# A 31-tap convolution on TensorE: from two token phases to four, in an eight-core encoder block

## The chip, the cores and the metric

The kernel runs as one program on all 8 cores of one Trainium2 chip, each core on its own sequences and with no exchange between cores. The time is the device time of the slowest core, in microseconds (us); lower is better.

## What is computed

A pre-normalised mixer layer, applied to 8 long sequences (8192 tokens) and 32 short ones (2048 tokens) of width 1024. One input projection of 3584 columns feeds two groups of 512 channels; their outputs are joined, projected back, gated and added to the residual, and a last RMSNorm follows.

```python
h = rmsnorm(x, norm_g) * (1.0 + scale[:, None, :]) + shift[:, None, :]
p = h @ w_in                                              # (B, L, 3584)
a_in, a_b, a_c, a_z, b_v, b_g, b_z = jnp.split(p, SPLITS, axis=-1)
y_a = a_b * dwconv(a_c * a_in, conv_a_w) * jax.nn.silu(a_z)          # 3 taps
u = b_v * jax.nn.sigmoid(b_g)
u = dwconv(u, conv_b_w) + conv_b_b                                   # 31 taps, each channel by itself
y_b = jax.nn.silu(head_layernorm(u, ln_g, ln_b)) * jax.nn.silu(b_z)  # norm over groups of 64 channels
y = jnp.concatenate([y_a, y_b], axis=-1) @ w_out                     # (B, L, 1024)
out = rmsnorm(x + gate[:, None, :] * y, final_g)
```

## The kernel before

**Windows and periods.** A core has 16 windows of 1024 tokens: eight of its long sequence, then two for each of four short ones. A window's tokens are split by parity into q = 0 and q = 1, 512 each. Period w of the loop does the input projection of window w, and beside it the long convolution, the norm and the output projection of window p = w - 1. Period 0 and `period_last` (w = 15, which also finishes its own window) have code of their own.

**Slots.** The order of work on every engine is written out by hand. A period has 28 slots; each slot is two `mm1` calls (L521), and each of these is 8 matmuls of 128 x 128 weights and 512 columns (L525). Slots 0 to 7 give the gated product u, 8 to 15 the input of the short convolution, 16 to 19 and 24 to 27 its gates, 20 to 23 the gate of group B (`zb`). After slot 21 comes `stage_d(p, 0)`, after slot 27 `stage_d(p, 1)`: the output projection (L757), 64 matmuls each. Two dictionaries hang further work on the slots: `mid` runs between the two `mm1` of a slot, `post` behind the slot. Each engine works its queue in order.

**The long convolution.** u is written to DRAM (`u_scratch`, L554), with 8 edge columns to the neighbouring windows (the halo; for a window with two neighbours one DMA, L561, otherwise L565). `vread(p, j)` reads it back as V, so that a row of V holds one channel at one shift: 16 channels x 8 shifts make the 128 rows; two DMAs of 64 rows each (L638). There are two V buffers; `vread` of j = 0 and 1 is issued after slots 4 and 5, of j = 2 and 3 after the first burst of convolution matmuls. `conv_b` (L642) does one of eight units u: 4 steps x 4 column positions, each 32 columns of weights (16 channels x 2 phases) against 512 tokens (L648). Four units (`conv4`) follow on each other as one burst of 64 matmuls, after slot 9 and after slot 15. Unit u needs V(u // 2).

**The norm.** ACT copies a unit's result with its bias to `sq` (L656), DVE adds four units (`add4`, L663), one matmul with Bn gives the mean (L671), DVE centres (L680), ACT squares, DVE adds, one matmul with Bm gives the variance (L689). ACT takes Ln and Exp (L698, L699), DVE multiplies (L709), ACT does silu (L712), POOL multiplies by the gate in YP (L714). `norm_hooks` (L831) sets the slots.

**Moves.** `g_move` (L583) brings the gate from `gst` to YP in the row order of the convolution, `y_move` (L726) the product from YP to yB in the order of the output projection. Both issue on SP, as do the loads of x (L308, L736), the transposes of the scaled rows to hT (L345), the stores of y (L813) and, in the periods 2 to 9, the preparation of gated output weights. `conv_a` (L594) is the short convolution: four operations of 512 columns on DVE. The squares of the last norm are ACT's (L786), and DVE's L795 and POOL's L797 wait for them.

## Time and profile before

| | us |
|---|---|
| median of 3 runs | 2233.69 (2232.13 to 2260.23) |
| the profiled execution | 2235.12 |
| its slowest core, from first to last instruction | 2233.5 (cores: 2220.0 to 2233.5) |
| PE busy | 2165.8 |
| DVE busy | 1326.2 |
| ACT busy | 980.0 |
| POOL busy | 628.2 |

The profile is that of core 3. PE (TensorE) is the busiest engine by far; a matmul's own duration (380 ns for 512 columns) includes its run through the array, and a stream of them steps faster than that. So the time of a stream is read from the starts of its first matmul and of the next line's first. "SPq" and "ACTq" rows are DMA issues on these engines' queues; their landing times stand in the answers on a line. A wait is put down to what ended last by the profile.

### The profile page before, as it was taken

The page shows a single profiled execution, that of the slowest core. Times are in us where ns is not written, and L with a number is a line of the kernel's source. Part 1 is how long each engine was busy: PE and PEld are TensorE (multiplying, and loading weights), DVE is VectorE, ACT ScalarE, POOL GpSimd, SP SyncE. Part 2 cuts the span into 40 slices and gives each one's busy share as a digit, 9 for nine tenths or more (in the row PEclk, how much of TensorE's full clock was granted, in tenths as well). Part 3 has the DMA queues.
Part 4 walks back from the last instruction along what each step waited for, and adds up shares of the span by engine and source line. Part 5 has one row for each costly group of instructions (what it writes and reads, how often), then busy time and mean ns, then how long its engine had stood idle before and what let it go on. Part 6 is the DMA issues. An engine that isn't in the chain of part 4 may idle for free.

```text
span 2233.5 us, 38878 instructions; the slowest of 8 cores (2220.0 to 2233.5 us)
## 1 busy us (share of the span) xinstructions
PE 2165.8 (97%) x11524; PEld 963.5 (43%) x11524; DVE 1326.2 (59%) x2251; ACT 980.0 (44%) x1644; POOL 628.2 (28%) x564
## 2 busy tenths in 40 slices
PE   4998999999999999999999999999999999999997
PEld 1443444444444444444444444444444444444443
DVE  1245574656657556476655747566575665647578
ACT  2232626345263443535435263443626445263464
POOL 3223324223242331423313242131311312122123
PEclk9999999999999999999999999999999999999999
DMA  9977477786766878668676777567565766656666
GB/s 259 155 212 192 131 186 197 201 199 183 190 188 197 212 183 175 174 191 236 180 202 175 195 229 209 153 185 171 168 187 154 195 196 155 187 128 204 159 180 223
DMA packets 300314, 418.49 MB, mean 187 GB/s; under 512 B 168616, under 2 KB 225104, under 8 KB 291920
## 3 DMA queue, kind: packets, MB, share of 16 engines
q1 hardware_dynamic: 291712, 408.50, 68.0%
q0 software_dynamic: 7392, 7.34, 2.6%
q8 instruction: 101, 1.65, 0.3%
q14 instruction: 101, 0.83, 0.1%
q10 hardware_dynamic: 1008, 0.17, 0.0%
HBM read 265.43 MB, written 92.82 MB: 160 GB/s over the span
## 4 chain that ended last, share of the span: by engine, by line
PE 88%; DMA 6%; DVE 2%; issue 1%; SPq 1%; ACT 1%; POOL 0%; DVEq 0%; POOLq 0%; ACTq 0%
PE pb L525 64%; PE pb L757 19%; PE pb L648 4%; DMA xb<-w_out 3%; DMA u_scratch<-u 1%; DMA V<-w_ada 1%; DMA w_in_sb<-w_in 1%; DVE sq L663 1%; SPq L393 0%; ACT sq L656 0%; PE pb L671 0%; PE pb L689 0%; DVE hT L386 0%; SPq L345 0%; DVE xb L810 0%
## 5 line engine op out<-in xcount | busy, mean ns | idle before, releaser
L525 PE MATMUL pb<-hT,w_in_sb 128*128 128x512 bf16 x7168 | 1578.5, 380 | 16.6 <-DMA w_in_sb<-w_in 9.7
L525 PEld LDWEIGHTS pb<-hT,w_in_sb 128*128 128x128 bf16 x7168 | 699.3, 98 | 875.9 <-issue 46.6
L531 ACT ACTIVATE tp<-pb 128x512 f32<-128x512 f32 x384 | 227.0, 595 | 618.3 <-PE pb L525 566.8
L768 DVE TENSOR_TENSOR xb<-pb,xb 128x512 f32<-128x512 f32 x252 | 171.4, 689 | 197.2 <-PE pb L757 185.3
L786 ACT ACTIVATE tp<-xb 128x1024 bf16<-128x1024 f32 x126 | 133.4, 1059 | 314.0 <-DVE xb L768 218.6
L757 PE MATMUL pb<-w_out_sb,yB 128*128 128x512 bf16 x960 | 251.2, 379 | 4.5
L757 PE MATMUL pb<-w_out_sb,yA 128*128 128x512 bf16 x960 | 246.3, 379 | 3.0 <-DVE xb L768 1.9
L797 POOL TENSOR_TENSOR rsE<-msE,mhalf 128x1 f32<-128x1 f32 x128 | 139.5, 1090 | 385.8 <-DVE msE L795 368.4
L324 POOL TENSOR_TENSOR rsA<-msA,mhalf 128x2 f32<-128x2 f32 x64 | 46.2, 722 | 649.9 <-DVE msA L322 649.9
L605 DVE SCALAR_TENSOR_TENSOR tp<-t,caT_sb,tp 128x512 f32<-128x512 bf16 x256 | 195.3, 763 | 28.4 <-DVE tp L602 1.4
L534 DVE TENSOR_TENSOR t<-pb,tp 128x512 bf16<-128x512 f32 x128 | 88.3, 690 | 160.7 <-PE pb L525 116.2
L714 POOL TENSOR_TENSOR YP<-tp,YP 128x512 bf16<-128x512 f32 x128 | 149.2, 1198 | 120.6 <-ACT tp L712 120.6
L316 ACT ACTIVATE tp<-xb 128x1024 bf16<-128x1024 f32 x128 | 134.9, 1055 | 95.9 <-DMA xb<-x 76.2
L551 DVE SCALAR_TENSOR_TENSOR u<-tp,pb 128x512 bf16<-128x512 f32 x128 | 87.7, 685 | 142.2 <-PE pb L525 141.8
L810 DVE SCALAR_TENSOR_TENSOR xb<-xb,rsE,fg_bc 128x1024 f32<-128x1024 f32 x125 | 162.7, 1303 | 6.2 <-POOL rsE L797 4.2
L329 POOL TENSOR_SCALAR xs<-xb,rsA 128x1024 bf16<-128x1024 f32 x128 | 144.6, 1141 | 14.7 <-POOL rsA L324 14.7
L663 DVE TENSOR_TENSOR sq<-sq 128x512 bf16<-128x512 bf16 x192 | 98.7, 527 | 82.5 <-ACT sq L656 75.6
L757 PEld LDWEIGHTS pb<-w_out_sb,yB 128*128 128x128 bf16 x960 | 91.8, 98 | 124.7 <-issue 18.4
L757 PEld LDWEIGHTS pb<-w_out_sb,yA 128*128 128x128 bf16 x960 | 93.7, 98 | 116.8 <-issue 4.2
L534 DVE TENSOR_TENSOR ga<-pb,tp 128x512 bf16<-128x512 f32 x128 | 87.6, 685 | 70.4 <-PE pb L525 64.5
L680 DVE SCALAR_TENSOR_TENSOR pb<-pb,cbb_sb,tp 128x512 f32<-128x512 f32 x128 | 87.5, 752 | 63.6 <-ACT tp L673 63.6
L503 POOL TENSOR_TENSOR xb<-xb 128x1024 bf16<-128x1024 f32 x32 | 76.9, 2408 | 147.9 <-DMA xb<-w_out 147.9
(102 smaller groups left out, 1308.2 us busy)
## 6 DMA issues: line engine op xcount, KB each, us to landing
xb<-x SPq DMA_DIRECT2D x254, 512.0 KB, 7.9
V<-u_scratch SPq DMA_DIRECT2D x128, 527.5 KB, 9.0
y<-xb SPq DMA_DIRECT2D x126, 512.0 KB, 3.9
xb<-w_out SPq DMA_DIRECT2D x40, 512.0 KB, 12.8
YP<-gst SPq DMA_DIRECT2D x64, 256.0 KB, 5.0
yB<-YP SPq DMA_DIRECT2D x120, 128.0 KB, 3.0
u_scratch<-u SPq DMA_DIRECT2D x80, 130.0 KB, 3.6
wg_scratch<-xb SPq DMA_DIRECT2D x32, 256.0 KB, 9.5
```

Source lines behind the costliest of these rows:

```text
L316: T.op("scalar", lambda e: e.activation(out=jb[:].bitcast(BF16), in_=xbuf[:], func=AF.Square, accum_out=ssA[:, c:c + 1]), reads=[xkey], wr ...
L329: T.op("gpsimd", lambda e, xbuf=xbuf, sub=sub, r=r: e.tensor_scalar(out=xs[:, sub, :], in0=xbuf[:], scalar1=rsA[:, r:r + 1], scalar2=1.0, ...
L525: T.op("tensor", lambda e, bank=bank, kc=kc: e.matmul(bank[:], lhsT=w_in_sb[:, kc, col0:col0 + 128], rhs=hT2[q][:, kc, :], start=(kc == 0) ...
L531: T.op("scalar", lambda e: e.activation(out=t[:], in_=bank[:], func=func, scale=scale), reads=[bkey], writes=[tkey])
L534: T.op("vector", lambda e: e.tensor_tensor(out=dst, in0=bank[:], in1=t[:], op=ALU.mult), reads=[tkey, bkey], writes=[dkey])
L605: T.op("vector", lambda e, k=k: e.scalar_tensor_tensor(out=acc[:], in0=terms[k], scalar=caT[:, j * KA + k:j * KA + k + 1], in1=acc[:], op0 ...
L714: T.op("gpsimd", lambda e, t=t, u=u: e.tensor_tensor(out=YP[:, u, :], in0=t[:], in1=YP[:, u, :], op=ALU.mult), reads=[tkey, ("yp", u, 0), ...
L757: T.op("tensor", lambda e, kc=kc, src=src: e.matmul(bank[:], lhsT=src, rhs=w_out_sb[:, kc, h * NT:(h + 1) * NT], start=(kc == 0), stop=(kc ...
L768: T.op("vector", lambda e, bank=bank, xbuf=xbuf, h=h: e.tensor_tensor(out=xbuf[:, h * NT:(h + 1) * NT], in0=bank[:], in1=xbuf[:, h * NT:(h ...
L786: T.op("scalar", lambda e: e.activation(out=jb[:].bitcast(BF16), in_=xbuf[:], func=AF.Square, accum_out=ssE[:, c:c + 1]), reads=[xkey], wr ...
L797: T.op("gpsimd", lambda e: e.tensor_tensor(out=rsE[:, c:c + 1], in0=msE[:, c:c + 1], in1=mhalf[:, 0:1], op=ALU.pow), reads=[("msE", c), "m ...
L810: T.op("vector", lambda e: e.scalar_tensor_tensor(out=xbuf[:], in0=xbuf[:], scalar=rsE[:, c:c + 1], in1=fg_bc[:], op0=ALU.mult, op1=ALU.mult),
```

## The change

**Four phases.** Tokens are split by their remainder mod 4. V holds 8 channels x 16 shifts in its rows, a matmul's 32 weight columns are 8 channels x 4 phases, and it covers 256 tokens. A unit is now 2 halves x 3 steps x 4 column positions, 24 matmuls of 256 columns; a burst (`conv_quad`) is 96. All four banks of a burst are taken first, and the four copies by ACT stand behind all matmuls; the bias is no longer added there but, centred beforehand, in `ln_center` (`center_bias` in period 0).

**Places.** The bursts stand after slots 8 and 14. The mean of the first stays two slots behind its burst and that of the second goes half a slot further behind; the second `add4` and all that follows come one slot later against the burst, so that they end at slots 15 and 21 as before.

**DMAs.** A V load is four pieces of 32 rows instead of two of 64. u goes out as two pieces per row, the halo is 4 columns for each of them, and a window with two neighbours has two halo DMAs. `y_move` is 16 DMAs of 64 KB a window instead of 8 of 128 KB, half of a quad's in `mid`, half in `post`. `g_move` is 16 DMAs of 64 KB on ACT's queue instead of 4 of 256 KB on SP's.

**Smaller operands.** Mean, variance, Ln, Exp and their copies have 256 columns. `add4` has one more addition of 256 columns; centring and silu are done in halves; `conv_a` has five operations (two of 512 columns, two of 256, one of 512). The ring TP has 4 buffers instead of 6, beside a new ring MR of two half-size ones; the ring of u has 3 instead of 4. Some constants of the start share memory with yA, and the table of taps loaded at the start is 384 KB instead of 128 KB.

The core of the diff (the host's reordering of channels, the constants and `period_last` are left out; of the two bursts that `period_last` has for its own window the second goes half a slot earlier, and the norm of both goes up to one output step later):

```diff
 def second_of(kind, w, q, j):
-                sides = ([] if wfirst[w] else [(w - 1, PAD + NT, PAD)]) + ([] if wlast[w] else [(w + 1, 0, NT)])
-                if len(sides) == 2:
...
+                sides = ([] if wfirst[w] else [(w - 1, PAD + NB, PAD)]) + ([] if wlast[w] else [(w + 1, 0, NB)])
+                for k, (ww, c, m) in enumerate(sides):
+                    T.dma("sync", lambda e, ww=ww, c=c, m=m: e.dma_start(out=u_rows(ww, q, j, c, PAD), in_=ub[:, :, m:m + PAD]),
+                          reads=[ukey], writes=[("Uh", q, j, w, ww)], semkey=("uh", ww > w) + ukey)
 def g_move(q):
-            for h in range(2):
-                T.dma("sync", lambda e, h=h: e.dma_start(out=YP[q::2, h::2, :], in_=gst[64 * h:64 * h + 64, :, :]),
+            for u in range(8):
+                T.dma("scalar", lambda e, u=u: e.dma_start(out=YP[q::2, u, :], in_=gst[32 * (u % 4):32 * (u % 4) + 32, 2 * (u // 4):2 * (u // 4) + 2, :]),
 def vread(p, j):
+            for b in range(4):
+                k = b
+                src = U_d[p, j]
+                src = bass.AP(src.tensor, src.offset + k, [[VN, 32], [1, VN - k]])
+                T.dma("sync", lambda e, b=b, k=k, src=src: e.dma_start(
+                    out=buf[32 * b:32 * b + 32, :, :].rearrange("p g t -> p (g t)")[:, 0:VN - k], in_=src),
+                    reads=deps, writes=[(key, b)], semkey=("vl", key, b))
+        def conv_quad(p, hh):
+            us = quad(hh)
...
+                cst[u] = list(PB.next(pin=True))
+            for u, h, a, g in itertools.product(us, range(2), range(3), range(4)):
+                vb, vkeys = V[u]
+                bank, bkey = cst[u]
+                j, G = u // 2, 8 * (u % 2) + 4 * h + g
+                T.op("tensor", lambda e, vb=vb, bank=bank, g=g, h=h, a=a, j=j, G=G: e.matmul(
+                    bank[32 * g:32 * g + 32, NB * h:NB * h + NB], lhsT=WC[:, 64 * a + 16 * j + G, :], rhs=vb[:, G * VW + 4 * a:G * VW + 4 * a + NB],
+                    start=(a == 0), stop=(a == 2), tile_position=(0, 32 * g)),
+                    reads=[("WC", 2 * a + j // 2)] + vkeys, writes=[bkey], signal=(a == 2 and h == 1 and g == 3))
...
+                T.op("scalar", lambda e, bank=bank, vv=vv: e.activation(out=vv[:], in_=bank[:], func=AF.Copy), reads=[bkey], writes=[vvkey])
 def norm_hooks(hh, h, mid, post):
             add(mid, h + 1, lambda: add4(quad(hh)))
-            add(mid, h + 2, lambda: conv_mean(hh))
-            add(mid, h + 2, lambda: ln_center(hh))
-            add(mid, h + 3, lambda: add4(quad(hh)))
-            add(mid, h + 4, lambda: ln_var(hh), lambda: ln_act(hh))
-            add(mid, h + 5, lambda: fin2(hh, 0))
-            add(post, h + 5, lambda: fin2(hh, 1))
+            add(post if hh else mid, h + 2, lambda: conv_mean(hh), lambda: ln_center(hh))
+            add(mid, h + 4, lambda: add4(quad(hh)))
+            add(post, h + 5, lambda: ln_var(hh), lambda: ln_act(hh))
+            add(mid, h + 6, lambda: fin2(hh, 0))
+            add(post, h + 6, lambda: fin2(hh, 1))
 def conv_hooks(p, mid, post):
             add(post, 4, lambda: vread(p, 0))
             add(post, 5, lambda: vread(p, 1))
-            for hh, h in enumerate((9, 15)):
-                add(post, h, lambda hh=hh: conv4(p, hh))
+            for hh, h in enumerate((8, 14)):
+                add(post, h, lambda hh=hh: conv_quad(p, hh))
                 if hh == 0:
                     add(post, h, lambda: vread(p, 2), lambda: vread(p, 3))
                 norm_hooks(hh, h, mid, post)
-                add(post, h + 6, lambda hh=hh: y_move(hh, yb))
+                add(mid, h + 7, lambda hh=hh: y_move(quad(hh)[:2], yb))
+                add(post, h + 7, lambda hh=hh: y_move(quad(hh)[2:], yb))
```

On PE, one period from its first slot on, before (L525 are the projection's matmuls, 8 for half a slot; L648 the convolution; L671 and L689 mean and variance):

```order
L525 MATMUL pb<-hT,w_in_sb 128x512 x224
L648 MATMUL pb<-V,WC 32x512 x64
L525 MATMUL pb<-hT,w_in_sb 128x512 x24
L671 MATMUL pb<-sq,Bn 128x512
L525 MATMUL pb<-hT,w_in_sb 128x512 x32
L689 MATMUL pb<-sq,Bm 128x512
L525 MATMUL pb<-hT,w_in_sb 128x512 x40
L648 MATMUL pb<-V,WC 32x512 x64
L525 MATMUL pb<-hT,w_in_sb 128x512 x24
L671 MATMUL pb<-sq,Bn 128x512
L525 MATMUL pb<-hT,w_in_sb 128x512 x32
L689 MATMUL pb<-sq,Bm 128x512
```

and after, where the same lines are L545, L677, L703 and L723:

```order
L545 MATMUL pb<-hT,w_in_sb 128x512 x208
L677 MATMUL pb<-V,WC 32x256 x96
L545 MATMUL pb<-hT,w_in_sb 128x512 x24
L703 MATMUL pb<-sq,Bn 128x256
L545 MATMUL pb<-hT,w_in_sb 128x512 x56
L723 MATMUL pb<-sq,Bm 128x256
L545 MATMUL pb<-hT,w_in_sb 128x512 x16
L677 MATMUL pb<-V,WC 32x256 x96
L545 MATMUL pb<-hT,w_in_sb 128x512 x32
L703 MATMUL pb<-sq,Bn 128x256
L545 MATMUL pb<-hT,w_in_sb 128x512 x48
L723 MATMUL pb<-sq,Bm 128x256
```

Each burst stands 16 matmuls of 512 columns earlier and has 96 entries. Counted from the burst's end, the first mean stays 24 behind, the second goes from 24 to 32, and both variances stand farther behind their means.

On SP, in a period whose window has two neighbours, around the loads for the first burst, before (L554 writes u, L561 the halo to both sides, L638 loads V, L308 loads x; L491 and L497 prepare output weights):

```order
L554 DMA u_scratch<-u 128x512
L561 DMA u_scratch<-u 128x2x8
L638 DMA V<-u_scratch 64x1x4220 x2
L554 DMA u_scratch<-u 128x512
L561 DMA u_scratch<-u 128x2x8
L638 DMA V<-u_scratch 64x1x4220 x2
L308 DMA xb<-x 128x1024
L554 DMA u_scratch<-u 128x512
L561 DMA u_scratch<-u 128x2x8
L491 DMA xb<-gate_scratch 128x1024
L497 DMA xb<-w_out 128x1024
L554 DMA u_scratch<-u 128x512
```

and after (L579, L583, L663, in the same order of names):

```order
L579 DMA u_scratch<-u 128x2x256
L583 DMA u_scratch<-u 128x2x4 x2
L663 DMA V<-u_scratch 32x4224
L663 DMA V<-u_scratch 32x4223
L663 DMA V<-u_scratch 32x4222
L663 DMA V<-u_scratch 32x4221
L579 DMA u_scratch<-u 128x2x256
L583 DMA u_scratch<-u 128x2x4 x2
L663 DMA V<-u_scratch 32x4224
L663 DMA V<-u_scratch 32x4223
L663 DMA V<-u_scratch 32x4222
L663 DMA V<-u_scratch 32x4221
```

V(0) and V(1) keep their places among the writes of u, as four issues each.

On ACT, after slot 21 and through the first output projection, after the change (L597 is the gate of group B, L602 `g_move`, L821 the squares of the last norm):

```order
L597 ACTIVATE gst<-pb 128x2x256 x2
L602 DMA YP<-gst 64x1x512 x8
L821 ACTIVATE tp,ssE<-xb 128x1024 x4
L597 ACTIVATE gst<-pb 128x2x256 x4
L602 DMA YP<-gst 64x1x512 x8
L551 ACTIVATE tp<-pb 128x512
```

The eight issues of `g_move` stand ahead of the four squares, where before ACT had none: there SP issued `g_move` as two DMAs behind the transposes.

## Rows read from the trace of the kernel before

**Rows 1.** The page: busy time by engine; the chain that ended last, by engine

```profile
PE 2165.8 (97%) x11524; PEld 963.5 (43%) x11524; DVE 1326.2 (59%) x2251; ACT 980.0 (44%) x1644; POOL 628.2 (28%) x564
PE 88%; DMA 6%; DVE 2%; issue 1%; SPq 1%; ACT 1%; POOL 0%; DVEq 0%; POOLq 0%; ACTq 0%
```

**Rows 2.** Waits of PE: line waited for, us in total, times, longest

```profile
PE pb L671 <- DVE sq L663: 8.4, 4, 2.6
PE pb L525 <- DVE hT L386: 5.9, 3, 2.6
```

**Rows 3.** Timeline of PE, period 7: start, us, line, operands, count

```profile
1034.64 8.80 PE L525 MATMUL pb<-hT,w_in_sb 128*128 128x512 bf16 x40
1043.37 3.64 PE L648 MATMUL pb<-V,WC 128*32 128x512 bf16 x64
1046.94 3.41 PE L525 MATMUL pb<-hT,w_in_sb 128*128 128x512 bf16 x15
```

**Rows 4.** Matmul groups by form: count, busy us, mean ns, idle before, releasers

```profile
L671 PE MATMUL pb<-sq,Bn 128*128 128x512 bf16 x32 | 12.1, 379 | 8.5 <-DVE sq L663 8.4 <-PE pb L525 0.2
...
L359 PE MATMUL pb<-yA,xs 128*128 128x128 bf16 x64 | 4.9, 219 | 0.3
```

**Rows 5.** Weight loads by form, same columns

```profile
L648 PEld LDWEIGHTS pb<-V,WC 128*32 128x32 bf16 x2048 | 51.8, 97 | 62.3 <-issue 13.6
...
L359 PEld LDWEIGHTS pb<-yA,xs 128*128 128x128 bf16 x64 | 3.8, 97 | 4.4 <-issue 3.9
```

**Rows 6.** Timeline of PE at the start, transposes

```profile
66.46 0.61 PE L359 MATMUL pb<-yA,xs 128*128 128x128 bf16 x8
```

**Rows 7.** Timeline of SP's DMA issues, period 10

```profile
1398.72 0.42 SPq L565 DMA_DIRECT2D u_scratch<-u  x1
...
1402.83 1.26 SPq L638 DMA_DIRECT2D V<-u_scratch  x2
...
1406.23 1.29 SPq L638 DMA_DIRECT2D V<-u_scratch  x2
```

**Rows 8.** V loads: first bursts of periods 1 and 15, second of period 6

```profile
L638 SPq DMA_DIRECT2D V<-u_scratch x4: 523/574/1007, 190.7 to 195.1; - x4
...
DMA to landing us min/median/max: 5.0/7.8/8.5
...
L638 SPq DMA_DIRECT2D V<-u_scratch x4: 520/529/567, 2068.6 to 2072.7; - x4
...
DMA to landing us min/median/max: 5.1/6.7/8.5
...
L638 SPq DMA_DIRECT2D V<-u_scratch x4: 515/518/851, 885.5 to 892.2; - x4
...
DMA to landing us min/median/max: 11.6/13.2/14.2
```

**Rows 9.** Timeline of PE, the bursts that needed these loads

```profile
205.69 3.64 PE L648 MATMUL pb<-V,WC 128*32 128x512 bf16 x64
...
2083.73 3.64 PE L648 MATMUL pb<-V,WC 128*32 128x512 bf16 x64
...
905.80 3.64 PE L648 MATMUL pb<-V,WC 128*32 128x512 bf16 x64
```

**Rows 10.** Timeline of SP's DMA issues, end of period 0

```profile
163.22 1.25 SPq L583 DMA_DIRECT2D YP<-gst  x2
164.66 6.78 SPq L345 DMA_TRANSPOSE hT<-xs  x4
```

**Rows 11.** Timeline of ACT: a DMA issue at the start; first square of period 9

```profile
17.08 0.59 ACTq L246 DMA_DIRECT2D lnb_sb<-lnbT  x1
...
1343.22 1.06 ACT L786 ACTIVATE tp<-xb 128x1024 bf16<-128x1024 f32 x1 [7.79 <-DVE xb L768]
```

**Rows 12.** Timelines of SP and of PE at the end

```profile
2200.64 3.00 SPq L726 DMA_DIRECT2D hT<-YP  x4
...
2205.76 3.18 PE L757 MATMUL pb<-w_out_sb,hT 128*128 128x512 bf16 x14
```

**Rows 13.** DVE groups by form, the long operation of the short convolution

```profile
L605 DVE SCALAR_TENSOR_TENSOR tp<-t,caT_sb,tp 128x512 f32<-128x512 bf16 x256 | 195.3, 763 | 28.4 <-DVE tp L602 1.4
```

More of the change, by code:

```diff
@@ L1 @@
 import contextlib
+import itertools
 import numpy as np
@@ L255, in build_nc @@
         T.op("gpsimd", lambda e: e.memset(ones1[:], 1.0), writes=["ones1"])
[L256 to L260 removed]
+        T.op("vector", lambda e: e.memset(scT, 0.0), writes=["scT"])
+        for i in range(3):
             T.op("gpsimd", lambda e, i=i: e.memset(UR.bufs[i][:], 0.0), writes=[("u", i)])
@@ L434, in gate_piece @@
                 gate_st["bank"] = PB.next(pin=True)
-                gate_st["bias"] = TP.next(pin=True)
+                gate_st["bias"] = (early[:, 256:512], "gbias")
                 bb, bk = gate_st["bias"]
@@ L632, in vread @@
             T._need("sync", T._deps("sync", [], VK["V%d" % key[1]]))
-            for par in range(2):
-                q = 1 - par
-                deps = [("U", q, j, p)] + ([] if wfirst[p] else [("Uh", q, j, p - 1)]) + ([] if wlast[p] else [("Uh", q, j, p + 1)])
-                src = U_d[p, par, j]
-                src = bass.AP(src.tensor, src.offset + par, [[VN, 16], [1, 4], [1, VN - 4]])
-                T.dma("sync", lambda e, par=par, src=src: e.dma_start(
-                    out=buf[64 * par:64 * par + 64, :, :].rearrange("p g t -> p (g t)")[:, 0:VN - 4], in_=src),
-                    reads=deps, writes=[(key, par)], semkey=("vl", key, par))
@@ L642, in conv_b @@
-        def conv_b(p, u):
-            j, hl = u // 2, u % 2
-            vb, vkey = vst[(p, j)]
-            bank, bkey = PB.next(pin=True)
-            for s in range(4):
-                for g in range(4):
-                    T.op("tensor", lambda e, s=s, g=g: e.matmul(
-                        bank[32 * g:32 * g + 32, :], lhsT=WC[:, (4 * u + g) * 4 + s, :], rhs=vb[:, 4 * hl + g, 4 * s:4 * s + NT],
-                        start=(s == 0), stop=(s == 3), tile_position=(0, 32 * g)),
-                        reads=[("WC", u // 2)] + [(vkey, k) for k in range(2)], writes=[bkey], signal=(s == 3 and g == 3))
-            if hl == 1:
-                VR.unpin(vkey)
-                vst.pop((p, j))
-            vv, vvkey = sqr.next(pin=True)
-            T.op("scalar", lambda e: e.activation(out=vv[:], in_=bank[:], func=AF.Identity, bias=cbb[:, u:u + 1], scale=1.0),
-                 reads=[bkey, "cbb"], writes=[vvkey])
-            cst[u] = [bank, bkey, vv, vvkey]
+            deps = []
@@ new lines, in vread @@
+            for q in range(2):
+                deps += [("U", q, j, p)] + ([] if wfirst[p] else [("Uh", q, j, p - 1, p)]) + ([] if wlast[p] else [("Uh", q, j, p + 1, p)])
+            for b in range(4):
[5 more added lines that the diff above has]
+                    reads=deps, writes=[(key, b)], semkey=("vl", key, b))
@@ L663, in add4 @@
                 T.op("vector", lambda e, x=x, y=y: e.tensor_tensor(out=x[:], in0=x[:], in1=y[:], op=ALU.add), reads=[xk, yk], writes=[xk])
+            x, xk = a
+            for n in (NB,):
+                T.op("vector", lambda e, n=n: e.tensor_tensor(out=x[:, 0:n], in0=x[:, 0:n], in1=x[:, n:2 * n], op=ALU.add), reads=[xk], writes=[xk])
         def quad(hh):
@@ L670, in conv_mean @@
             mb, mbk = PB.next()
-            T.op("tensor", lambda e: e.matmul(mb[:], lhsT=Bn[:], rhs=vv[:], start=True, stop=True), reads=["Bn", vvkey], writes=[mbk])
-            m, mkey = TP.next(pin=True)
-            T.op("scalar", lambda e: e.activation(out=m[:], in_=mb[:], func=AF.Copy), reads=[mbk], writes=[mkey])
+            T.op("tensor", lambda e: e.matmul(mb[:, 0:NB], lhsT=Bn[:], rhs=vv[:, 0:NB], start=True, stop=True), reads=["Bn", vvkey], writes=[mbk])
+            m, mkey = MR.next(pin=True)
+            T.op("scalar", lambda e: e.activation(out=m[:], in_=mb[:, 0:NB], func=AF.Copy), reads=[mbk], writes=[mkey])
             cst[("m", hh)] = (m, mkey)
@@ L688, in ln_var @@
             vb, vbkey = PB.next(pin=True)
-            T.op("tensor", lambda e: e.matmul(vb[:], lhsT=Bm[:], rhs=vv[:], start=True, stop=True), reads=["Bm", vvkey], writes=[vbkey])
+            T.op("tensor", lambda e: e.matmul(vb[:, 0:NB], lhsT=Bm[:], rhs=vv[:, 0:NB], start=True, stop=True), reads=["Bm", vvkey], writes=[vbkey])
             for u in quad(hh):
```

326 lines of the change are left out of this document (178 added, 148 removed).

## The prediction

> **What bounds the kernel now.** I read the page first: PE is busy 97% of the span and the chain that ended last is 88% PE [rows 1], so time is gained only by shortening PE's stream or by taking away what it waits for. The list of PE's waits comes next: outside the start, PE waits for the sums ahead of the mean matmul and for the modulated rows hT [rows 2]. The timeline of a steady period then shows PE running without a gap: 40 matmuls of 512 columns from 1034.64 to 1043.37 us, 0.218 us each, then the 64 convolution matmuls, 3.57 us from the first to the next line's first [rows 3]. So a term counts fully if it lies in PE's stream, and anything else only once PE has to wait for it.
>
> **The convolution, 64 x 512 columns to 96 x 256.** Four matmuls with different column positions run together: 64 matmuls in 3.57 us are 16 groups of four at about 0.216 us, and 3.57 - 16 x 0.216 = 0.12 us around the burst. So four tiles together cost what one 512-column matmul costs. For 256 columns there is no row in bf16. The nearest is the transposes of 128 columns: eight in 0.61 us, of which the last alone has 219 ns [rows 4, 6], so (0.61 - 0.219) / 7 = 56 ns each. Halfway between 56 (128 columns) and 216 (512) by column count, 56 + (216 - 56) / 3 = 109, say 110 ns. The new burst has 24 groups: 24 x 0.110 + 0.12 = 2.76 us, 0.81 less; 32 bursts give **-25.9 us**. The bound on the other side is a group that takes its weight load in full: the loads of this line take 97 ns each [rows 5], 97 + 110 = 207 ns a group, 24 x 0.207 + 0.12 = 5.09 us, +1.52 x 32 = +48.6. The saving is zero at 16 x 0.216 / 24 = 144 ns a group. I take 110, because the transposes, each with a weight load of 97 ns of its own, step at 56 ns [rows 5, 6]: loads overlap there even where they are longer than the matmul.
>
> The page of the Trainium skill "TensorE: Matmul & The Clock Gate", Part 3, "The mechanism", speaks against the change: a weight load overlaps running matmuls only where the row group differs, and here every load uses all 128 rows. By that rule the burst would be the 5.09 us of the upper bound. The present trace does not follow it: transposes on all 128 rows step faster than one load lasts.
>
> **Mean and variance.** The 32 mean matmuls [rows 4] and as many variance matmuls go from 512 to 256 columns: 64 x (0.216 - 0.110) = **-6.8 us**. Their operands are one addition longer on DVE.
>
> **Waits for the sums.** The 8.4 us in four waits [rows 2] average 2.1. They stand at the second burst of periods with w_out preparation, where the mean now comes half a slot (8 matmuls of 0.216, 1.73 us) later against its burst; one more half-size addition eats some 0.3. Left are about 4 x 0.7: **-5** (0 to -8.4).
>
> **Start of period 1.** On SP the transposes (164.66 us) stood behind g_move (163.22, two issues of 0.6) [rows 10], and PE waits 5.9 us for their rows [rows 2]. g_move is now on the ACT queue, and the transposes no longer stand behind its wait: **-4** (0 to -8).
>
> **V loads, the new exposure.** Bursts move up one slot (16 x 0.216 = 3.45 us); V(0) and V(1) are still issued after slots 4 and 5, in the middle of the u writes [rows 7], and the data is as late as before. V(1) is needed by the third of four units. Before, that was 1.73 us behind the burst's start; now it is 3.45 earlier plus two units of 6 groups, 12 x 0.110 = 1.31: 2.14 us *before* the old start. Last landings against the old start: in period 1 195.1 + 8.5 = 203.6 against 205.69, -2.1; in period 15 2072.7 + 8.5 = 2081.2 against 2083.73, -2.5 [rows 8, 9]; all fifteen, read the same way: -2.1, -0.4, -0.9, -1.1, -1.3, +0.9, -1.8, -2.5, -1.7, -1.9, -1.4, -1.9, -2.2, -1.4, -2.5. On top come 0.47 us for the second halo DMA ahead of it on SP (0.42 each plus the step) [rows 7] in periods 1 to 6, and an estimated 0.3 because the last of four issues of some 0.55 replaces the last of two, in a queue that is backed up 8 us anyway. Wait = landing + delay + 2.14, where positive: 12.7 us in periods 1 to 6, 4.9 after: **+17.6**. Bounds: 9 if the delays are nil and the four pieces land sooner; 35 if every early period is like the sixth (6 x 3.8) and the others lose 1.3 each. PE's stream is in order, so nothing else fills these waits.
>
> The second burst moves as well. Its loads follow the first burst's release of V and usually land some 8 us ahead, but in period 6 the last lands at 892.2 + 14.2 = 906.4 at most (905.6 by its own issue) against 905.80 [rows 8, 9]. Four such periods (2, 3, 5, 6) could lose up to 2.9 each, 9.6 together; most of it is the same backlog that the first burst's wait already gave time to drain: **+3.5**.
>
> **Moved DMA issues.** g_move on ACT is 16 issues a window of 0.4 to 0.6 us [rows 11]. The first eight are queued behind slot 21's activations and ahead of four squares; ACT idled 7.79 us before the first of these (1343.22) [rows 11]. Four units can go at once, 2.4 us; the other four wait for y_move's landing, some 3 us after its last issue, and end near 1343.4: covered, barely. The second eight stand ahead of slot 24's copies, 4.8 us in which PE fills three of eight banks. Behind the first stand the squares, DVE's scale of them waits for these, and PE would wait for banks only after that. Taken as **0** (0 to +15, one us a period). y_move has 16 issues instead of 8; its first half goes out half a slot earlier, and the transposes behind it have all of slots 22 to 27 as cover: 0. conv_a gains one half-size operation on DVE, about 0.4 us of L605's 763 ns [rows 13] against a slot of 3.45; DVE is 59% busy, so it delays the last u by up to 1 us, which is inside the V range. The split of silu and of the centring adds instructions on ACT (44%) and DVE, with no PE wait near it.
>
> **Tail.** The last window's y_move issues 3.00 us for four and PE continues at 2205.76 [rows 12]; eight issues are twice that, partly under 40 matmuls: **+3** (0 to 5).
>
> **Sum** against the profiled execution (2235.1 us, its slowest span 2233.5): -25.9 - 6.8 - 5 - 4 + 17.6 + 3.5 + 0 + 3 = -17.6, so 2217.5. The median of the runs is 1.4 below the profiled execution: **2216**.
>
> **Rivals.** *A, the V loads are covered after all*: 32-partition pieces land sooner, or a wait in one period lets the queue catch up for all later ones. For it: late periods have only 0 to 1 us to find. Against it: the loads are bound by the queue, and that moves the same bytes. Without the two V terms: 2216 - 21.1 = 2195. *B, the V loads take everything*: both bursts wait at their upper bounds (35 + 9.6), 2195 + 44.6 = 2240. For it: periods 2 to 6, where landings already come within a microsecond of the old start. Against it: from period 7 on PE has no other wait and the queue drains. *C, slower: the four-tile group does not get below 207 ns*, because weight loads or the issue of instructions set its pace. It decides at 144 ns. For it: a group is eight instructions, at 216 ns 27 ns each, and no row has a sustained pace above that; 110 ns needs 14. Against it: transposes step at the column count. 2216 + 25.9 + 48.6 = 2290; mean and variance stand alone among 512-column matmuls and keep their gain.
>
> **How the numbers follow.** Forecast (2203 to 2230) 0.66; A (2186 to 2203) 0.15; B (2230 to 2252) 0.13; C (2265 to 2300) 0.06. A change of 2%, about what a measurement of this kernel can tell from none, is 45 us: below 2189 or above 2278. Only the lower end of A is below, 0.05; C, for nearly all its width, is above, 0.06; the rest, 0.89, is in between. The range leaves out C, the lower end of A and the upper end of B: 2191 to 2243.
>
> **What would show it.** In the profile after: a burst of 96 with 2.76 us to the next line's first matmul (C: over 5); mean and variance steps of 0.11; a new line in PE's waits, convolution <- DMA V, of 15 to 20 us on the slowest core, mostly periods 1 to 6 (A: under 3; B: over 35, and on both bursts); the waits for sq and hT at half or less; late periods shorter by two bursts and four norm matmuls, 2 x 0.81 + 4 x 0.106 = 2.0 us, less the V wait. I am wrong if the squares on ACT start late by microseconds and PE then waits on banks, or if u itself comes late from DVE so that the V issues, not the landings, slip.

## The result and the profile after

The changed kernel takes 2365.72 us (median of 3 runs, 2364.77 to 2670.41) against 2233.69: **132 us slower**. The ratio is 1.055 with an interval of 1.0373 to 1.0726. The interval is wide because one of the three runs was disturbed and is left out. The forecast was 2216 (2191 to 2243), with 0.06 for slower.

The page after, busy time by engine and the chain that ended last, to be read against [rows 1]:

```profile
PE 2180.0 (92%) x12550; PEld 1005.6 (43%) x12550; DVE 1391.8 (59%) x2568; ACT 976.1 (41%) x1772; POOL 627.4 (27%) x564
PE 70%; DMA 15%; DVE 4%; SPq 4%; issue 3%; ACT 2%; POOL 0%; DVEq 0%; ACTq 0%; POOLq 0%
PE pb L545 49%; PE pb L792 18%; DMA V<-u_scratch 6%; DMA u_scratch<-u 5%; PE pb L677 3%; DMA xb<-x 2%; SPq L663 2%; DMA V<-w_ada 1%; DVE tp L628 1%; DVE sq L692 1%; DMA w_in_sb<-w_in 1%; DVE u L575 1%; SPq L579 1%; ACT sq L686 1%; SPq L583 1%
```

PE is no longer the whole chain: 15% of it is DMA, and the two transfers in it are u into DRAM and V out of it. The waits of PE (line waited for, us in total, times, longest), to be read against [rows 2], name the same pair:

```profile
PE pb L677 <- DMA V<-u_scratch: 87.3, 23, 8.5
PE pb L703 <- DVE sq L695: 13.6, 8, 4.2
PE pb L545 <- ACT tp L551: 12.2, 5, 4.2
PE pb L545 <- DVE hT L394: 7.5, 1, 7.5
PE pb L677 <- ACT tp L551: 3.8, 5, 1.0
```

The wait for V was forecast as 15 to 20 us; it is 87 on the slowest core (58 to 87 over the eight). The compute steps came out as worked out. This is PE's timeline (start, us, line, operands, count) of a second burst without stalls, where [rows 3, 9] show the old one:

```profile
1543.64 0.27 PE L723 MATMUL pb<-sq,Bm 128*128 128x256 bf16 x1
1543.75 3.62 PE L545 MATMUL pb<-hT,w_in_sb 128*128 128x512 bf16 x16
1547.30 2.81 PE L677 MATMUL pb<-V,WC 128*32 128x256 bf16 x96
1550.04 2.33 PE L545 MATMUL pb<-hT,w_in_sb 128*128 128x512 bf16 x10
```

The burst lasts 1550.04 - 1547.30 = 2.74 us (forecast 2.76), so a group of four tiles steps at about 110 ns; the variance matmul steps at 1543.75 - 1543.64 = 0.11 us.

**Where the time went**, slowest core against slowest core (2364.0 - 2233.5 = 130.5 us). PE's waits for V: +87.3. Waits for banks that ACT had not freed (L551, both lines): +16.0. Waits for sq: 13.6 - 8.4 = +5.2. Waits for hT rows: about +3. PE's own busy time: 2180.0 - 2165.8 = +14.2, although the burst and the norm became shorter. That is 126 of 130.5. The last term is the clock. In this table of PE's stretches on core 3 (stretch, length, busy, matmuls; granted clock, DMA share, GB/s), the stretch from 499.2 begins inside a stall of 7.20 us that lasts until 503.7:

```profile
490.00:499.00 9.00, 6.05 (x70) 1.00 1.06 152
499.20:509.30 10.10, 5.59 (x55) 0.50 0.99 205
509.40:515.00 5.60, 5.60 (x28) 1.00 0.95 173
```

PE's timeline of the same stretch (idle before and its releaser in brackets):

```profile
495.01 1.49 PE L677 MATMUL pb<-V,WC 128*32 128x256 bf16 x48 [0.45 <-DMA V<-u_scratch]
503.71 2.75 PE L677 MATMUL pb<-V,WC 128*32 128x256 bf16 x48 [7.20 <-DMA V<-u_scratch]
506.39 6.80 PE L545 MATMUL pb<-hT,w_in_sb 128*128 128x512 bf16 x24
```

PE first stood, then got 0.50 of full speed (1.2 of 2.4 GHz): its second half burst took 2.75 us for 48 matmuls where the first took 1.49. From 85 us on, stretches at 0.50 sum to 72 to 126 us a core after, and 12 to 23 before. The transfers around the stall keep the 16 engines busy throughout (shares of 1.06 and 0.99).

**Why V is late.** The rows of DMA issues give landing times (the last column, median us from issue to landing). Before:

```profile
u_scratch<-u SPq DMA_DIRECT2D x80, 130.0 KB, 3.6
u_scratch<-u SPq DMA_DIRECT2D x48, 128.0 KB, 4.8
u_scratch<-u SPq DMA_DIRECT2D x80, 2.0 KB, 3.3
u_scratch<-u SPq DMA_DIRECT2D x48, 4.0 KB, 4.6
```

After:

```profile
DMA packets 347188, 419.12 MB, mean 177 GB/s; under 512 B 199080, under 2 KB 271824, under 8 KB 338768
u_scratch<-u SPq DMA_DIRECT2D x80, 130.0 KB, 5.9
u_scratch<-u SPq DMA_DIRECT2D x48, 128.0 KB, 9.8
u_scratch<-u SPq DMA_DIRECT2D x176, 2.0 KB, 8.6
```

u holds two blocks of 256 columns a row now, so its pieces are 512 bytes instead of 1024 and those of the halo 8 instead of 16: the trace counts 22,528 packets of 16 bytes before and 45,056 of 8 bytes after. Bytes are the same, but u and its halo land in 6 to 10 us instead of 3 to 5. V itself lands no later after its issue (9.0 us before, 6.5 to 9.2 for its four pieces after); late against the burst, which itself comes a slot sooner, is its issue. SP waits for the halo before it may issue V, as it did before: its waits for u and halo sum to 90.5 us on core 3 before and 112.3 on core 5 after. Its timeline on core 5, to be read against [rows 7]:

```profile
495.93 0.88 SPq L583 DMA_DIRECT2D u_scratch<-u  x2
502.17 1.72 SPq L663 DMA_DIRECT2D V<-u_scratch  x4
503.99 0.38 SPq L579 DMA_DIRECT2D u_scratch<-u  x1
504.42 0.99 SPq L583 DMA_DIRECT2D u_scratch<-u  x2
505.68 1.72 SPq L663 DMA_DIRECT2D V<-u_scratch  x4
```

and PE's:

```profile
494.78 12.68 PE L545 MATMUL pb<-hT,w_in_sb 128*128 128x512 bf16 x58
512.13 2.75 PE L677 MATMUL pb<-V,WC 128*32 128x256 bf16 x48 [4.67 <-DMA V<-u_scratch]
```

After its halo issues SP stands from 496.81 to 502.17, then V(0), the next u and V(1) leave late, and PE waits 4.67 us for V(0) and 4.78 for V(1). Each piece of V now reads rows of both parities and so waits for the halo of both. That by itself moves nothing: before, the half of V that SP issues first waited for the odd parity, which is written last. The ring of u adds to it: in all, DVE waits 32.6 us for u buffers whose transfers haven't landed, where the row of before has no such wait.

### The profile page after: what moved, and what is told of

It is laid out like the page before. It is cut to its first block, busy times and chain, and to the rows that moved or that the text cites. A ratio compares the mean times of both kernels' runs of the same rounds, so it can differ in the third digit from the quotient of the medians.

```text
span 2364.0 us, 43369 instructions; the slowest of 8 cores (2334.0 to 2364.0 us)
## 1 busy us (share of the span) xinstructions
PE 2180.0 (92%) x12550; PEld 1005.6 (43%) x12550; DVE 1391.8 (59%) x2568; ACT 976.1 (41%) x1772; POOL 627.4 (27%) x564
## 2 busy tenths in 40 slices
DMA packets 347188, 419.12 MB, mean 177 GB/s; under 512 B 199080, under 2 KB 271824, under 8 KB 338768
## 4 chain that ended last, share of the span: by engine, by line
PE 70%; DMA 15%; DVE 4%; SPq 4%; issue 3%; ACT 2%; POOL 0%; DVEq 0%; ACTq 0%; POOLq 0%
PE pb L545 49%; PE pb L792 18%; DMA V<-u_scratch 6%; DMA u_scratch<-u 5%; PE pb L677 3%; DMA xb<-x 2%; SPq L663 2%; DMA V<-w_ada 1%; DVE tp L628 1%; DVE sq L692 1%; DMA w_in_sb<-w_in 1%; DVE u L575 1%; SPq L579 1%; ACT sq L686 1%; SPq L583 1%
## 5 line engine op out<-in xcount | busy, mean ns | idle before, releaser
L545 PE MATMUL pb<-hT,w_in_sb 128*128 128x512 bf16 x7168 | 1590.8, 383 | 32.8 <-ACT tp L551 12.2
L545 PEld LDWEIGHTS pb<-hT,w_in_sb 128*128 128x128 bf16 x7168 | 701.5, 98 | 894.2 <-issue 80.8
L551 ACT ACTIVATE tp<-pb 128x512 f32<-128x512 f32 x384 | 226.4, 594 | 636.4 <-PE pb L545 504.1
L821 ACT ACTIVATE tp<-xb 128x1024 bf16<-128x1024 f32 x126 | 133.2, 1057 | 298.3 <-DVE xb L803 210.0
L628 DVE SCALAR_TENSOR_TENSOR tp<-t,caT_sb,tp 128x256 f32<-128x256 bf16 (+2 forms) x384 | 228.2, 594 | 41.8 <-DVE tp L625 1.4
L677 PE MATMUL pb<-V,WC 128*32 128x256 bf16 x3072 | 114.0, 310 | 91.4 <-DMA V<-u_scratch 87.3
L337 ACT ACTIVATE tp<-xb 128x1024 bf16<-128x1024 f32 x120 | 126.4, 1054 | 84.2 <-DMA xb<-x 65.4
L677 PEld LDWEIGHTS pb<-V,WC 128*32 128x32 bf16 x3072 | 90.5, 108 | 118.0 <-issue 112.1
```

The costliest lines, as they stand in the source:

```text
L545: T.op("tensor", lambda e, bank=bank, kc=kc: e.matmul(bank[:], lhsT=w_in_sb[:, kc, col0:col0 + 128], rhs=hT2[q][:, kc, :], start=(kc == 0) ...
L551: T.op("scalar", lambda e: e.activation(out=t[:], in_=bank[:], func=func, scale=scale), reads=[bkey], writes=[tkey])
L628: T.op("vector", lambda e, k=k, dst=dst, src=src: e.scalar_tensor_tensor(out=dst, in0=src, scalar=caT[:, j * KA + k:j * KA + k + 1], in1=d ...
L677: T.op("tensor", lambda e, vb=vb, bank=bank, g=g, h=h, a=a, j=j, G=G: e.matmul(bank[32 * g:32 * g + 32, NB * h:NB * h + NB], lhsT=WC[:, 64 ...
L821: T.op("scalar", lambda e: e.activation(out=jb[:].bitcast(BF16), in_=xbuf[:], func=AF.Square, accum_out=ssE[:, c:c + 1]), reads=[xkey], wr ...
```

## Experiments

All ratios are to the kernel before, from runs on the same chip. Theories at the start: the earlier slots alone (the forecast's own term, larger than estimated); the u path, by SP's queue, by the V pieces, by the wait for both parities' transfers, or by the traffic of the small pieces; and the smaller rings (tp 6 to 4 with 2 small ones, u 4 to 3).

**Slots.** The change with its bursts back at 9 and 15, and the kernel before with its bursts at 8 and 14 (the hooks of the norm go with the slots):

```
-            for hh, h in enumerate((8, 14)):      # after_s915; norm_hooks as before
+            for hh, h in enumerate((9, 15)):
-            for hh, h in enumerate((9, 15)):      # before_s814; norm_hooks as in the change
+            for hh, h in enumerate((8, 14)):
```

> The change with its bursts back at slots 9 and 15 and the norm hooks of before (mean two slots, variance four slots behind the burst, y_move six); layout, pieces, queues and rings stay. Theory 1, the moved slot: every wait of the convolution for V shrinks by up to the slot, 3.45 us; the 60 to 90 us of these waits fall to 5 to 25 (periods 1 to 6 only), the low-clock stretches behind them go too, and the time falls to 2215 to 2270. Theory 2, the new data path (u, halo and V arrive microseconds later than the old ones, whatever the slot): waits of 3 to 4 us stay in most periods, 40 us or more in all, and the time stays over 2290. Theory 3, the smaller rings: waits for ACT's copies stay at 10 to 27 us, and the time stays over 2300.

> The kernel before with one thing changed: its bursts at slots 8 and 14 and the norm hooks of the change behind them (y_move still after slots 15 and 21). Theory 1, the moved slot alone costs what was seen: 60 us or more of waits for V, time over 2300. Theory 2, it is the new data path: by the landings of before, 15 to 25 us of waits for V, time 2245 to 2265. If V is hidden in the old layout: within 5 us of 2234.

Measured 1.0353 (1.0319 to 1.0387) and 1.012 (1.008 to 1.0161). In the kernel before, the earlier slot makes waits for V of 12.2 us on the slowest core, below the 21.1 of the forecast; in the change, most of the loss stays at the old slots. First the row of before_s814, then that of after_s915:

```profile
PE pb L648 <- DMA V<-u_scratch: 12.2, 6, 4.0
```

```profile
PE pb L677 <- DMA V<-u_scratch: 33.1, 10, 5.2
PE pb L703 <- DVE sq L695: 23.6, 9, 4.9
```

**Rings of the change in the kernel before** (tp 4 with two buffers for mean and rstd, u 3):

> The kernel before with the rings of the change: four buffers of tp and two of full size for mean and reciprocal instead of six for both, three buffers of u instead of four (gate bias and the squares of period 0 in yA1's memory, as in the change). Theory 3, the rings: a new line of PE waits for ACT's copies into tp, 10 us or more, time 2250 to 2270. Theories 1 and 2: within 8 us of 2234.

Measured 1.0041 (1.0004 to 1.0077). By themselves the rings cost the old kernel about 9 us (1 to 17).

**The pieces of V.** after_v128 loads V(j) by one DMA of 128 rows (and a tail), after_v64 by two of 64 rows:

```
+ full = bass.AP(src.tensor, src.offset, [[1, 4], [VN, 32], [1, VN - 3]])            # after_v128
+ half = bass.AP(src.tensor, src.offset + 2 * b, [[VN, 32], [1, 2], [1, n]])         # after_v64
```

> The change with V read by one DMA of 128 rows (4221 of 4224 columns) and a small one for the last three columns of the first 32 rows, instead of four DMAs of 32 rows; the bytes stay. Theory 4, pieces of 32 rows are slow: the second V lands 2 us sooner after its issue, waits for V fall by 20 to 35 us and the time to 2300 to 2330. Otherwise, if the pieces don't matter: within 10 us of 2366; one DMA that has to land whole may be later by up to 1 us a load, 2375.

> The change with V read by two DMAs of 64 rows, 32 runs outermost and two shifts inside, plus a small one for the last two columns, instead of four DMAs of 32 rows; the rows' order in V and in the table of weights follows. Theory 4, pieces of 32 rows are slow: the second V lands 1 to 2 us sooner, time 2325 to 2350. If pieces don't matter: within 10 us of 2366. Against the one DMA of 128 rows, whose outermost level has four steps (2869): if it was the number of outermost steps that spreads a load over the engines, this one with 32 steps must be back at 2380 or less.

Measured 1.2846 (1.2807 to 1.2885), 2864 us, with this row, and 1.0566 (1.049 to 1.0643), 2356 us:

```profile
PE pb L678 <- DMA V<-u_scratch: 330.4, 32, 16.5
```

The same bytes in one DMA with an outermost level of four steps wait 330 us; in two with 32 steps they cost what the change costs, within an interval of 34 us. So the size of V's pieces is not the cause.

**SP's queue.** s915_uact issues u and halo on ACT's queue instead of SP's, with the bursts at 9 and 15:

```
-  T.dma("sync", ...)     # u rows and halo
+  T.dma("scalar", ...)
```

> The change at slots 9 and 15 (after_s915) with the writes of u and of the halo issued on ACT's queue instead of SP's. Theory 2, these small writes are late because they stand in SP's ring behind stores of 512 KB and loads of V: on a ring of their own they land in 3 to 4 us, SP never stands in front of a V load, waits for V and for the sums fall under 15 us, time 2210 to 2245. Rival: ACT stands in its queue until DVE has written u, its copies come late, and PE waits for them; time 2290 or more. If the ring doesn't matter: within 10 us of after_s915 (2300).

Measured 1.0417 (1.0396 to 1.0438) against 1.0353 on SP. u and halo land about as late from another queue, so it is not SP's ring that makes them late. The run doesn't clear SP's issuing of all blame: on the slowest cores PE's wait for V falls from 33.1 to 20.2 us, while its waits for hT go from 9.0 to 26.0 and those for ACT's copies from 1.8 to 6.4, as the rival had it. Landings:

```profile
u_scratch<-u ACTq DMA_DIRECT2D x80, 130.0 KB, 6.0
u_scratch<-u ACTq DMA_DIRECT2D x48, 128.0 KB, 6.7
u_scratch<-u ACTq DMA_DIRECT2D x176, 2.0 KB, 6.8
```

**The u path alone.** before_upath gives the kernel before, in windows with two neighbours, u in two pieces of 512 bytes a row and two halo DMAs:

> The kernel before, slots and rings as they were, with u written in the pieces of the change in the six windows with two neighbours: two pieces of 512 bytes a row (the buffer has a gap between them) and two halo DMAs instead of one (16-byte pieces). Theory 2a, small pieces make u and halo late: their landing goes from 4 to 5 us in periods 2 to 6 to 8 to 10, SP stands in front of the V loads until they land, 20 to 40 us of new waits for V and for the sums, time 2255 to 2275. If pieces and number of DMAs don't matter: within 8 us of 2234.

Measured 1.0109 (1.0087 to 1.013): 24 us, by the same sign (u lands later, V is waited for). The halo has its 22,528 pieces of 16 bytes here as before; only u's pieces and the DMAs of the halo double in these windows. So u can land late without more or smaller pieces of the halo:

```profile
PE pb L655 <- DMA V<-u_scratch: 14.7, 5, 3.9
u_scratch<-u SPq DMA_DIRECT2D x48, 128.0 KB, 8.6
u_scratch<-u SPq DMA_DIRECT2D x176, 2.0 KB, 6.3
```

**The halo.** after_nohalo writes whole u rows with empty edges and no halo DMA, so the convolution lacks the neighbouring windows' columns. after_dummyhalo is the same with all halo DMAs issued into a scratch array that nobody reads:

```
-  sides = ...                                             # after_nohalo
-  for k, (ww, c, m) in enumerate(sides): T.dma("sync", ... out=u_rows(ww, q, j, c, PAD) ...)
+  lo, hi = 0, VW
-  ... out=u_rows(ww, q, j, c, PAD), in_=ub[:, :, m:m + PAD]      # after_dummyhalo, from after_nohalo
+  ... out=uh_rows(ww, q, j, c, PAD), in_=ub[:, :, m:m + PAD]
```

> The change without the halo: every window is padded with zeros as if it stood alone, no halo DMA is issued and V waits for none (the edges between windows are left out of the computation). Theory 2b, SP waits in front of the V loads until this period's halo has landed: periods 1 to 6 fall from 143 to 150 us to 134 to 138, time 2290 to 2320. Theory 1 alone (the loads themselves are too late for slot 8): V loads are issued where they were in the late periods and each period keeps 3 to 5 us of waits, 2320 to 2350. If the halo doesn't matter: over 2350.

> after_nohalo with the halo's DMAs issued again as in the change, same number, sizes and places on SP, but into a scratch tensor that nobody reads, so that no V load waits for them (the edges between windows are left out of the computation). Theory 2b, it is the wait of SP for this period's halo in front of the V loads: time as after_nohalo, 2260 to 2285. Theory 2c, it is the traffic of the small pieces itself: u's landing goes back from 4 to 6 to 10 us, periods 1 to 6 take over 142 us, time 2330 or more.

Measured 1.0177 (1.0149 to 1.0205), below both ranges expected, and 1.0475 (1.0453 to 1.0498). Without the halo, PE's wait for V on the slowest core is near the forecast (23.0 us, and 1.2 to 23.0 over the cores); the transfers alone, which nothing waits for but the u buffers, bring most of the time back. First after_nohalo, then after_dummyhalo:

```profile
PE pb L673 <- DMA V<-u_scratch: 23.0, 12, 3.6
u_scratch<-u SPq DMA_DIRECT2D x128, 132.0 KB, 3.9
```

```profile
PE pb L681 <- DMA V<-u_scratch: 49.2, 15, 5.7
u_scratch<-u SPq DMA_DIRECT2D x128, 132.0 KB, 5.9
```

So of 1.055, 0.037 (83 us) hang on the halo: 0.030 (66 us) on its traffic, and 0.0075 (17 us) on waiting for it. The interval of 1.055 is wide: the 83 us are good to about 40, and the 17 are not settled. With four u buffers (below), where the intervals are narrow, the halo costs 1.0448 - 1.014 = 0.031, 69 us.

**What in the traffic.** Three variants of after_dummyhalo: pieces of 64 bytes in the same number, one halo DMA instead of two in windows with two neighbours, and the same pieces into SBUF:

```
-  out=uh_rows(ww, q, j, c, PAD), in_=ub[:, :, m:m + PAD]
+  out=uh_rows(ww, q, j, 128 if c else 0, 32), in_=ub[:, :, ...32 columns]    # after_dummy64
+  for k, (ww, c, m) in enumerate(sides[:1]):                                 # after_dummyhalf
+  out=hsb[:, 4 * (2 * (ww > w) + q) + j], in_=ub[:, :, m:m + PAD]            # after_dummysb
```

> The kernel with the halo's values left out of the convolution (u rows written whole, the halo transfers kept into a scratch array that nobody reads), but each piece of those transfers is 64 bytes instead of 8, with the same number of pieces. If the price hangs on the number of pieces, the ratio to the kernel before stays at about 1.047 (1.040 to 1.055), u's 130 KB lands in about 5.9 us. If it hangs on pieces of 8 bytes being written as part of something wider, the ratio falls to about 1.02 to 1.03 and u lands in about 4 to 4.5 us.

> The same kernel with pieces of 8 bytes, but only one of the two halo transfers in the windows that have two neighbours, so half of the pieces there. If the price hangs on pieces, about half of the 3 points between the kernel without halo (1.0177) and the one with unread halo (1.0475) go: 1.028 to 1.037. If a few pieces are enough to hold the engines, it stays above 1.042.

> The same kernel with all halo transfers and pieces of 8 bytes, but written into an unread tile of SBUF instead of DRAM. If the price is that of short writes in DRAM, the ratio falls to about 1.02 to 1.025 and u lands in about 4 us. If it is that of the number of pieces, wherever they go, it stays at about 1.04 to 1.05.

Measured 1.0338 (1.0316 to 1.0361), 1.0325 (1.0273 to 1.0377) and 1.0343 (1.0255 to 1.0431). Wider pieces, another target or one DMA less each take off about half of the 0.030 between 1.0177 and 1.0475. No single answer holds, and the number of pieces is only suggested: after_dummyhalf has 32,768 instead of 45,056, but also 128 DMAs instead of 176. On cores 0, 1, 6 and 7 its excess over after_nohalo from burst to burst falls from 4.7 to 2.8 us in periods 2 to 6, where pieces and DMAs halve, but also from 2.7 to 2.0 in later ones, where neither changes. The landing of u does not order as the price does; in turn after_dummy64, after_dummyhalf, after_dummysb:

```profile
u_scratch<-u SPq DMA_DIRECT2D x128, 132.0 KB, 4.2
```

```profile
u_scratch<-u SPq DMA_DIRECT2D x128, 132.0 KB, 4.9
```

```profile
u_scratch<-u SPq DMA_DIRECT2D x128, 132.0 KB, 3.5
```

In after_dummysb u lands sooner than with no halo at all (3.5 against 3.9 us), and still the kernel takes 1.0343. What costs time there is not shown. An untested rival is the issue itself: in its timeline SP takes 1.29 us to issue the two halo DMAs of one u, ahead of V in the same queue, and all of these runs but after_dummyhalf keep every issue.

The Trainium skill, "DMA: Bandwidth & Descriptors", section "Why small descriptors are slow (HBM only)", says that short pieces carry a fixed overhead in transfers to or from HBM and that those between SBUFs don't suffer it. The ratio does fall with SBUF as the target (1.0475 to 1.0343, interval 1.0255 to 1.0431), but 1.0343 - 1.0177 remain, and pieces of 64 bytes that stay in DRAM bring as much (1.0338).

**Ring and slots, with and without halo.** Four u buffers (and one small statistics buffer less) in place of three:

```
-  UR = Ring("u", [... for i in range(3)], T);  MR = Ring("mr", [... for i in range(2)], T)
+  UR = Ring("u", [... for i in range(4)], T);  MR = Ring("mr", [... for i in range(1)], T)
```

> The change at slots 9 and 15 and without the halo (the edges between windows are left out of the computation). If slot and halo together are the whole loss, this shows the gain that the prediction took for the matmuls, 26 to 38 us: time 2195 to 2215. Rival, a third cause beside them (rings, u in half-size pieces, g_move on ACT's queue): 2225 or more.

> after_s915 with four buffers of u again instead of three (paid for by one buffer instead of two in the ring of mean and reciprocal). Theory 3a, u's late landing fills a ring of three and holds DVE in its queue, and with it the sums and hT: the 7 us wait at the start goes, waits for the sums fall from 25 to 30 us to 10 to 15, time 2260 to 2280. If the ring doesn't matter: within 8 us of after_s915 (2300).

> The changed convolution with its bursts at slots 9 and 15, without halo transfers (the edges of the convolution are left out), and with four u buffers again and one of the small statistics buffers less. If the u ring is the third cause, the ratio falls from 1.0067 to about 0.99 to 0.998 (2212 to 2230 us), since four buffers were worth about 1 point at slots 9 and 15 with the halo. If the halo's traffic was what kept the u buffers occupied, it stays at 1.003 to 1.009.

> The changed kernel with one thing undone: four u buffers again, and one of the two small statistics buffers less. At slots 9 and 15 four buffers took 1.0 point (1.0353 to 1.0249). If the ring's share is its own term, the same 1 point goes here: 1.040 to 1.047. If the ring matters only as part of the same V stalls, more goes: below 1.035.

> The change at its own slots 8 and 14 without halo transfers (the edges of the convolution are left out) and with four u buffers again, one small statistics buffer less. Slots alone cost 1.1 points without the halo (1.0177 against 1.0067), the ring 0.7 at slots 9 and 15 (1.0067 against 0.9994). If the terms add, this is 1.008 to 1.013. If the ring was what made V late at 8 and 14, it falls to 1.000 to 1.005.

| ratio to before | slots 8, 14 | slots 9, 15 |
|---|---|---|
| halo, 3 u buffers | 1.055 (the change) | 1.0353 |
| halo, 4 u buffers | 1.0448 (1.0431 to 1.0466) | 1.0249 (1.0224 to 1.0274) |
| no halo, 3 u buffers | 1.0177 | 1.0067 (1.0041 to 1.0092) |
| no halo, 4 u buffers | 1.014 (1.0119 to 1.016) | 0.9994 (0.9954 to 1.0033) |

Each is a term of its own: the halo 2.6 to 3.7 points, the slots (with the hooks of the norm) 1.1 to 2.0, the ring 0.4 to 1.0; the ring's 1.0 next to 1.055 lies inside that interval, and the slots' 2.0 and the ring's 0.4 are barely clear of theirs. With the halo, slots and ring cost more than without it, and it costs more with the new slots and three buffers. The ring also shows at the start. On core 3 of the change DVE waits for a u buffer, then scales the rows, and PE waits behind:

```profile
78.02 0.69 DVE L575 SCALAR_TENSOR_TENSOR u<-tp,pb 128x512 bf16<-128x512 f32 x1 [7.64 <-DMA u_scratch<-u]
78.62 1.89 DVE L394 TENSOR_SCALAR hT<-pb,gsT,shT 128x512 bf16<-128x512 bf16 x4
```

```profile
79.30 16.06 PE L545 MATMUL pb<-hT,w_in_sb 128*128 128x512 bf16 x66 [6.80 <-DVE hT L394]
```

With four buffers this wait is 0.8 us again; with three and no halo it is 3.2 to 5.0 over the cores.

**Earlier operands.** s915_early_ur4 puts u of both parities in turn earlier in the slot order (`ge[:2] + go[:2] + ge[2:] + go[2:]`) and the modulation of the odd parity's hT half a slot to a slot earlier, with four u buffers:

> s915_ur4 with the slots of u in another order, so that both parities of j = 0 and 1 are written in slots 0 to 3 instead of 0, 1, 3 and 4 (the modulation of hT1 half a slot to a slot earlier for it); V loads keep their slots, so the halo that they wait for is issued a slot earlier. Theory 2b: waits for V go nearly to nothing, time 10 to 30 us under s915_ur4. Rival: hT1 is not there by slot 2 and PE waits for it in every period, 1 to 2 us each; time 15 to 30 us over s915_ur4.

Measured 1.0275 (1.0249 to 1.0302), against 1.0249 without. On the slowest cores V's wait falls from 30.7 to 15.8 us and the norm's two grow from 27.5 to 42.8, by as much; rows of s915_early_ur4:

```profile
PE pb L723 <- DVE sq L695: 17.9, 7, 4.1
PE pb L677 <- DMA V<-u_scratch: 15.8, 6, 4.1
```

No variant of the change that computes the whole convolution was faster than the kernel before; the best is 1.0249.

## Why the prediction was wrong, step by step

- **The convolution (-25.9), mean and variance (-6.8): right.** 2.74 us against 2.76, steps of 0.11 us. PE's busy time shows most of it where V is not waited for: 2145.2 in s915_nohalo_ur4 for the same 12,550 matmuls, against 2165.8 before [rows 1], 20.6 less at a granted clock of 0.988 against 0.993. Rival C fell with it: the loads overlap. The rule of the Trainium skill, "TensorE: Matmul & The Clock Gate", Part 3, "The mechanism", lets no load overlap a matmul on the same rows. With the 97 ns of a load [rows 5] that would have made the group 207 ns; the trace shows 110.
- **V loads (+17.6 and +3.5): the step that failed.** It said that "the data is as late as before" and gave 0.47 us for the second halo DMA, its issue on SP. What was mis-sized is the data itself: I counted the halo's bytes and one more issue, and not what its transfers do to the others. u then lands 2 to 5 us later, SP stands until the halo has landed, and DVE waits for u buffers. The wait became 87.3 us in place of 21.1; with the halo taken out it is 23.0 and the kernel at 1.0177. Which property of the halo costs how much stays open: its pieces double and shrink to 8 bytes, its DMAs double where a window has two neighbours, and the runs that vary them don't single one out. That the 23.0 lie near 21.1 may be luck, since the eight cores have 1.2 to 23.0. Rival B had the direction; its price of 44.6 was bounded by landings of the old data. The text named the case "that the V issues, not the landings, slip", with u late from DVE; DVE is late in part, but because u's buffers come free late.
- **What follows a stall: missing.** The busy time of the same 12,550 matmuls is 2180.0 in the change and 2145.2 in s915_nohalo_ur4: 34.8 us, at a granted clock of 0.968 and 0.988 on the two cores. And a stalled burst releases V late: the next eight V issues and the x load behind them on SP slip, ACT waits for x, and PE for the banks that ACT would free. Core 1 of the change, ACT and then PE:

```profile
545.19 1.06 ACT L337 ACTIVATE tp<-xb 128x1024 bf16<-128x1024 f32 x1 [8.91 <-DMA xb<-x]
```

```profile
546.97 3.43 PE L545 MATMUL pb<-hT,w_in_sb 128*128 128x512 bf16 x8 [4.42 <-ACT tp L551]
```

  The stalls are only part of these bank waits (16.0 us on the slowest core of the change, 12.9 on that of after_nohalo); the slots bring them in. At slots 9 and 15 they are 1.7 to 2.5 us a core, even with waits for V of 33.1 (after_s915), and in before_s814 they are 4.6 to 9.2 with the old burst, none before. The forecast priced the new slots by V alone.
- **Waits for the sums (-5): wrong sign.** 13.6 us against 8.4, eight times instead of four. With hardly a wait for V it is the same (15.0 us in s915_nohalo). The later mean is not at fault: in before_s814, which has it with the old burst, these waits are 0.2 us or less. Nor are the copies, which got shorter (592 ns each against 691). They start late. Core 7 of s915_nohalo_ur4, where the burst ends at 366.77, DVE, ACT and PE:

```profile
367.12 0.69 DVE L739 TENSOR_TENSOR tp<-pb,mr 128x512 f32<-128x512 f32 x1 [5.08 <-POOL YP L746]
369.38 2.04 ACT L682 ACTIVATE sq<-pb 128x512 bf16<-128x512 f32 x4
374.57 0.27 PE L699 MATMUL pb<-sq,Bn 128*128 128x256 bf16 x1 [2.44 <-DVE sq L691]
```

  The last product of the first burst's norm waits for a tp buffer that POOL still reads, ACT's silu waits for the product, and the copies stand behind the silu. The ring tp has four buffers instead of six; no run gives the change six, so that the ring is the reason is argued, not shown.
- **Start (-4): wrong.** g_move left SP's queue as said, and the wait that it was to shorten went from 5.9 to 2.3 us on the slowest cores. But the u ring of three, which I did not cost, makes another of 6.4 to 9.7 us there over the cores, 0.8 before.
- **Moved issues on ACT (0), tail (+3): no sign against them.** No row of PE's waits leads to g_move's issues, and the wait on ACT is one for x, not for squares. At the tail PE waits 2.0 us for y_move's rows.
- **The sum.** Even with halo and ring taken out and the old slots kept, the kernel is at 0.9994 (rival A's 2195 would be 0.983). There steady periods take 131.3 to 131.5 us instead of 133.1 from burst to burst (forecast: 2.0 less); some 25 us of saving a core are given back by the waits for sq (about 15), a first burst 4 to 5 us later and lower clock (some 7). These are sizes read from core 0's trace, not taken apart by a run.

## What to carry to other kernels

A layout that halves a DMA's contiguous run is not costed by its bytes: count its pieces and its DMAs too, look above all at the smallest transfers, and at what waits for their landing. If in doubt, take them out of the kernel once and measure. A wait that moves to a new place on PE is dearer than its length: count the clock after it, and what the late release of its buffers holds up in the issuing queue. A saving on the busiest engine is only had where the engines that feed it keep the distance they had.
